# One encoder layer on one core: another tile order, another order of squares, scalings and loads in its output stage

## The reference, cut to what matters

```
u = rms_norm(x, g_norm);  z = u @ w_in             # q, k, v, g_att, xr, g_lru
o = diff_attention(q, k, v, ...)                   # 8 heads of 64
o_att = rms_norm(o per head, sub_norm) * (1 - lam_init)
o_lru = rg_lru_branch(xr, ...)                     # recurrences both ways
mix = concat([o_att * silu(g_att), o_lru * silu(g_lru)])
h = x + mix @ w_out
e = (p @ w_ple) * sigmoid(h @ w_pg)
y = h + rms_norm(e, g_ple)
```

## Time and profile before

| | |
|---|---|
| median of 3 runs | 1027.68 us (1026.09 to 1029.2) |
| the profiled execution | 1027.9 us, of which the span of the trace is 1026.1 us |
| granted TensorE clock, mean over the span | 0.993 |
| busy: PE / DVE / ACT / POOL | 97% / 66% / 62% / 47% |

### The profile page before, as it was taken

The page is one execution under the profiler, slowest core; times in us unless marked ns, Lnnn a source line. Parts: engine busy times, 40 slices in busy tenths (PEclk is TensorE's granted clock), DMA queues, the critical chain, the costliest instruction groups (busy, mean ns, idle before and its releaser), DMA issues.

```text
span 1026.1 us, 15666 instructions
## 1 busy us (share of the span) xinstructions
PE 990.3 (97%) x5720; PEld 785.2 (77%) x5720; DVE 679.0 (66%) x1117; ACT 636.8 (62%) x1051; POOL 482.8 (47%) x396
## 2 busy tenths in 40 slices
PE   8999999999999999989999999999989999999996
PEld 7867777777788888878777777777767887777775
DVE  4735857592583341579999999999848672444444
ACT  7748485846631231569999999999737443444442
POOL 1163343626656540155677676665610125555451
PEclk9999999999999999999999999999989999999999
DMA  9741543323255437659867666523457780222221
GB/s 345 273 142 36 174 149 104 118 82 134 72 177 184 142 95 204 212 158 234 208 195 173 149 188 173 132 93 124 171 168 239 230 280 10 72 74 81 86 73 68
DMA packets 106909, 154.55 MB, mean 151 GB/s; under 512 B 10313, under 2 KB 69193, under 8 KB 106825
## 3 DMA queue, kind: packets, MB, share of 16 engines
q1 hardware_dynamic: 106688, 153.55, 50.0%
q10 hardware_dynamic: 144, 0.00, 0.0%
HBM read 104.17 MB, written 46.20 MB: 147 GB/s over the span
## 4 chain that ended last, share of the span: by engine, by line
PE 66%; DVE 17%; issue 10%; ACT 3%; POOL 2%; DMA 2%; DVEq 0%; POOLq 0%; SPq 0%; ACTq 0%
DVE E_ L1899 10%; PE b_ps L2340 6%; PE b_ps L2342 6%; PE b_ps L2341 6%; PE b_ps L2202 6%; PE b_ps L2204 5%; PE b_ps L2203 5%; PE o_ps L2397 3%; PE s_ps L2353 3%; PE w_ps L2314 3%; PE uT_ps L2277 2%; DVE ratio L1908 2%; PE left_ps L2527 2%; PE left_ps L2530 2%; PE left_ps L2529 2%
## 5 line engine op out<-in xcount | busy, mean ns | idle before, releaser
L1381 ACT ACTIVATE E_<-E_,nmax 128x1024 f32<-128x1024 f32 (+1 forms) x184 | 186.6, 1018 | 13.2 <-DVE nmax L1899 13.2
L1899 DVE CUSTOM_DVE_ANT_0 E_<-s_ps,bias 128x1024 f32<-128x1024 f32 (+1 forms) x184 | 188.2, 1057 | 9.2 <-PE s_ps L2353 9.0
L1087 POOL TENSOR_TENSOR E_<-E_,ratio 128x576 f32<-128x576 f32 (+3 forms) x92 | 84.7, 920 | 92.6 <-DVE E_ L1915 92.6
L1090 POOL TENSOR_TENSOR E_<-E_ 128x576 f32<-128x576 f32 (+3 forms) x92 | 103.6, 1126 | 7.2
L2204 PE MATMUL b_ps<-u_hi,wA_lo 128*128 128x512 f32 x256 | 99.8, 390 | 0.0
L2353 PE MATMUL s_ps<-KL,QL 128*128 128x512 f32 x256 | 88.6, 430 | 8.1 <-DVE nmax L1899 8.0
L1396 ACT ACTIVATE WT<-w_ps 128x1024 f32<-128x1024 f32 (+1 forms) x96 | 83.5, 870 | 5.9 <-PE w_ps L2314 5.5
L2314 PE MATMUL w_ps<-ident,E_ 128*128 128x128 f32 x624 | 83.5, 273 | 2.1 <-ACT WT L1396 2.0
L2202 PE MATMUL b_ps<-u_hi,wA_hi 128*128 128x512 f32 x216 | 85.5, 396 | 0.0
L2314 PEld LDWEIGHTS w_ps<-ident,E_ 128*128 128x128 f32 x624 | 72.5, 140 | 15.2 <-issue 6.3
L2203 PE MATMUL b_ps<-u_lo,wA_hi 128*128 128x512 f32 x216 | 84.1, 389 | 0.0
(11 more groups left out here) (345 smaller groups left out, 2595.8 us busy)
## 6 DMA issues: line engine op xcount, KB each, us to landing
QL<-qk_t SPq DMA_DIRECT2D x32, 256.0 KB, 7.2
KL<-qk_t SPq DMA_DIRECT2D x32, 256.0 KB, 8.5
bias<-line_d SPq DMA_DIRECT2D x8, 960.0 KB, 12.1
x_sb<-in_x SPq DMA_DIRECT2D x12, 512.0 KB, 9.0
z_ch<-z_stage SPq DMA_DIRECT2D x24, 256.0 KB, 3.2
qk_t<-qh SPq DMA_DIRECT2D x24, 256.0 KB, 2.3
qk_t<-ql SPq DMA_DIRECT2D x24, 256.0 KB, 2.8
mf<-mix_t SPq DMA_DIRECT2D x24, 256.0 KB, 4.8
```

Of the source, the lines that this page charges most:

```text
L1090: gp.tensor_tensor(one, one, two, ALU.add).then_inc(w_gp, 1)
L1381: act.activation(e, e, ACT.Exp, bias=nmax[:, n % 5, c:c + 1], scale=-1.0, accum_out=sums[:, n % 5, c:c + 1]).then_inc(e_done, 1)
L1899: dve.tensor_tensor_reduce(weights_at(n)[:, c, 0:n_tok], s_ps[:, c, 0:n_tok], b[:, ::-1], -1.0, 3e38, ALU.add, ALU.min, nmax[:, n % 5, c:c ...
```

## The change

Places 2 and 3 swap tiles, so place 2 is now tile 2, a short and a `HALF` tile, and the banks follow. SP loads it before it stores the last attention output, and in each round issues `load_mix` ahead of `load_o`. ACT squares `n + 3` at the head of its round, and scales `n + 2` after `mix_high(n + 1)`, with the root just before; the small root that was there to have the table loaded is gone. In places 4, 6 and 8 PE transposes the next tile behind the `half_tile` products instead of ahead of them. POOL makes `sums_low(0)` ahead of the low parts of p, and one low part of w_ple ahead of its last `add_half`. In the gate loop DVE makes `joined(g - 1, 3)` ahead of `scaled_e(g - 1, 1)`. In the last pair the gain goes to another buffer and no longer waits for the square, and one sum is put off.

```
@@ -382,7 +382,7 @@
         wo_hi_done = sem("wo_hi_done"); wl_lo_done = sem("wl_lo_done"); wa_lo_done = sem("wa_lo_done")
         wg_in = [sem(f"wg_in{s}") for s in range(2)]
         wp_in = sem("wp_in"); wp_hi_done = sem("wp_hi_done"); wp_lo_done = sem("wp_lo_done")
-        SEQ = [0, 1, 8, 2, 9, 3, 10, 4, 11, 5, 6, 7]
+        SEQ = [0, 1, 2, 8, 9, 3, 10, 4, 11, 5, 6, 7]
         WHOLE = [SEQ.index(t) for t in range(8, NT)]
         HALF = [i for i in range(NT) if i not in WHOLE]
         IN_DRAM = NT - 4
@@ -458,8 +458,8 @@
 
         def mix_bank(i):
 
-            if i < 3:
-                return (h_ps[:], hq_ps[:], all_ps[:, 4:8:3, :])[i]
+            if i < 4:
+                return (h_ps[:], hq_ps[:], h_ps[:], all_ps[:, 4:8:3, :])[i]
             return h_ps[:] if i % 2 else hq_ps[:]
 
         ORDER = [PAIRS - 2, PAIRS - 1] + list(range(PAIRS - 2))
@@ -935,15 +935,16 @@
             for b in range(2):
                 sp.wait_ge(hp_out[b], 16 * IN_STEPS // 2)
             load_x_again(1)
+            load_o(2)
             store_o(1, HEADS // 2 - 1)
-            sp.wait_ge(o_st[1], 16 * 4)
-            load_o(2)
             load_mf(10)
             for n in range(NT):
+                if n + 2 < NT:
+                    load_mix(n + 2)
+                if n == 0:
+                    sp.wait_ge(o_st[1], 16 * 4)
                 if n + 3 < NT:
                     load_o(n + 3)
-                if n + 2 < NT:
-                    load_mix(n + 2)
                 if 1 <= n < NT - 1:
                     load_x_again(n + 1)
                     if n + 1 in HALF and HALF.index(n + 1) >= 2:
@@ -1117,15 +1118,19 @@
                 gp.tensor_tensor(hp_sb[:, k % 2, :], hp_sb[:, k % 2, :], x_rd[n % 2][:], ALU.add
                                  ).then_inc(fin["x_sum"], 1)
 
+            def embedding_low(k):
+                gp.wait_ge(wp_hi_done, k + 1)
+                gp.tensor_tensor(wp_lo[:, k, :], wp_raw[:, k, :], wp_hi[:, k, :].bitcast(F32),
+                                 ALU.subtract).then_inc(wp_lo_done, 1)
+
             o_scale(0)
             add_half(0)
             o_scale(1)
             for k in range(1, len(HALF)):
+                if k == len(HALF) - 1:
+                    embedding_low(0)
                 add_half(k)
-            for k in range(PC):
-                gp.wait_ge(wp_hi_done, k + 1)
-                gp.tensor_tensor(wp_lo[:, k, :], wp_raw[:, k, :], wp_hi[:, k, :].bitcast(F32),
-                                 ALU.subtract).then_inc(wp_lo_done, 1)
+            embedding_low(1)
 
             def sum_low(g, i, raw, pair):
                 gp.wait_ge(fin["s_hi"], 4 * g + i)
@@ -1154,10 +1159,10 @@
                 gp.tensor_tensor(e_sb[:, r, :], e_sb[:, r, :], h_sb[:, slot_of(g, r), :], ALU.add
                                  ).then_inc(fin["y_done"], 1)
 
+            sums_low(0)
             gp.wait_ge(fin["x_sum"], len(HALF))
             p_low(0, 1)
             p_low(0, 0)
-            sums_low(0)
             sum_low(0, 4, s4_raw, s4)
             for g in range(LAST):
                 if g:
@@ -1507,10 +1512,8 @@
 
             mix_high(0)
             heads_out(2 * HEADS - 1)
+            square_o(2)
             mix_high(1)
-            act.activation(mse[:, 0:1], neghalf[:, 0:1], ACT.Sqrt, scale=-2.0)
-            square_o(2)
-            root_o(2)
 
             def a21_copy(g):
                 act.wait_ge(fin["h_tr"], START["h_tr"] + 4 * g + 1)
@@ -1558,17 +1561,19 @@
                 act.activation(p_hi[:, r, :, :], p_sb[:, r, :, :], ACT.Copy).then_inc(fin["p_hi"], 1)
 
             for n in range(NT):
+                if n == 0:
+                    root_o(2)
+                    scale_o(2)
+                if n + 3 < NT:
+                    square_o(n + 3)
                 if 1 <= n < NT - 1:
                     mix_high(n + 1)
-                if n + 2 < NT:
+                if 1 <= n < NT - 2:
+                    root_o(n + 2)
                     scale_o(n + 2)
-                if n + 3 < NT:
-                    square_o(n + 3)
                 if n in (0, 1, 2, 3, 4, 6, 8):
                     gate_high({0: 0, 1: 1, 2: 2, 3: 3, 4: 4, 6: 5, 8: 6}[n])
-                if n + 3 < NT:
-                    root_o(n + 3)
-                if n == NT - 2:
+                if n == NT - 3:
                     for k in range(PC):
                         act.wait_ge(wp_in, 32)
                         act.activation(wp_hi[:, k, :], wp_raw[:, k, :], ACT.Copy).then_inc(wp_hi_done, 1)
@@ -2008,6 +2013,11 @@
                     row = x_rd[n % 2][:]
                 if n >= 4:
                     dve.wait_ge(fin[f"h_out{n % 2}"], 16 * min(n // 2, 4))
+                if n == 3:
+                    dve.tensor_tensor(h_sb[:, n, LEFT], mix_bank(n)[:, 0, :], row[:, LEFT], ALU.add)
+                    dve.tensor_tensor(h_sb[:, n, RIGHT], mix_bank(n)[:, 1, :], row[:, RIGHT], ALU.add
+                                      ).then_inc(fin["h_done"], 1)
+                    return
                 dve.tensor_tensor(h_sb[:, n % 4, :].rearrange("p (a b) -> p a b", a=2), mix_bank(n),
                                   row.rearrange("p (a b) -> p a b", a=2), ALU.add).then_inc(fin["h_done"], 1)
 
@@ -2061,9 +2071,9 @@
             mix_low(0)
             o_normalise(1)
             heads_scaled(2 * HEADS - 1)
+            mean_square(2)
             o_gate(1)
             mix_low(1)
-            mean_square(2)
             for n in range(NT):
                 if 1 <= n < NT - 1:
                     o_gate(n + 1)
@@ -2134,6 +2144,7 @@
             for g in range(PAIRS):
                 if g:
                     joined(g - 1, 3, "p2", right_ps[:], sg[0][:, LEFT])
+                    scaled_e(g - 1, 1)
                     gated_e(g - 1, 0)
                     scaled_e(g - 1, 0)
                 joined(g, 1, "p7", left_ps[:], sg[1][:, RIGHT])
@@ -2147,7 +2158,6 @@
                 gated_e(g, 1)
                 sum_four(g + 1)
                 a12_low(g + 1)
-                scaled_e(g, 1)
 
             def half_e(k, r, c, sigs):
                 dve.wait_ge(fin["sig"], 4 * LAST + sigs)
@@ -2157,18 +2167,18 @@
                                   ALU.mult).then_inc(fin["e_done"], 1)
 
             def half_gain(k, r, c):
-                dve.wait_ge(fin["esq"], 2 * LAST + k)
-                dve.tensor_tensor(e_sb[:, r, c], e_sb[:, r, c], gpB[:, c], ALU.mult).then_inc(fin["t_done"], 1)
+                dve.wait_ge(fin["e_done"], START["e_done"] + 2 * LAST + k)
+                dve.tensor_tensor(sg[r][:, c], e_sb[:, r, c], gpB[:, c], ALU.mult).then_inc(fin["t_done"], 1)
 
             def last_mean(r, one, two):
                 dve.wait_ge(fin["esq"], 2 * LAST + two)
                 dve.tensor_scalar(mse[:, r:r + 1], sse[:, 2 + one:3 + one], sse[:, 2 + two:3 + two], EPS, ALU.add,
                                   ALU.add).then_inc(fin["ems"], 1)
 
-            def last_sum(r):
+            def last_sum(r, parts):
                 dve.wait_ge(fin["ers"], START["ers"] + 2 * LAST + r + 1)
-                for c in (RIGHT, LEFT):
-                    dve.scalar_tensor_tensor(out=e_sb[:, r, c], in0=e_sb[:, r, c], scalar=rse[:, r:r + 1],
+                for c in parts:
+                    dve.scalar_tensor_tensor(out=e_sb[:, r, c], in0=sg[r][:, c], scalar=rse[:, r:r + 1],
                                              in1=h_sb[:, slot_of(LAST, r), c], op0=ALU.mult, op1=ALU.add
                                              ).then_inc(fin["y_half"], 1)
 
@@ -2182,11 +2192,12 @@
             half_gain(3, 0, LEFT)
             half_e(4, 1, LEFT, 4)
             dve.wait_ge(fin["t_done"], 2 * LAST + 3)
-            last_sum(0)
+            last_sum(0, (RIGHT,))
+            half_gain(4, 1, LEFT)
             last_mean(1, 1, 4)
-            half_gain(4, 1, LEFT)
+            last_sum(0, (LEFT,))
             dve.wait_ge(fin["t_done"], 2 * LAST + 4)
-            last_sum(1)
+            last_sum(1, (RIGHT, LEFT))
 
 
         @block.tensor
@@ -2468,11 +2479,12 @@
                 if n == 1:
                     pe.wait_ge(wt_done, NSTEP)
                     pe.wait_ge(o_done, 2 * HEADS)
-                if n >= 3:
-                    pe.wait_ge(fin["h_done"], 1 if n == 3 else n - 1)
+                if n == 2 or n >= 4:
+                    pe.wait_ge(fin["h_done"], {2: 1, 4: 2, 5: 3}.get(n, n - 1))
                 if n in WHOLE[1:]:
                     half_tile(2 * SEQ[n])
                     half_tile(2 * SEQ[n] + 1)
+                    turn_o(n + 1)
                 pe.wait_ge(fin["m_lo"], n + 1)
                 for b in range(2):
                     c = slice(b * 512, (b + 1) * 512)
@@ -2598,7 +2610,8 @@
             pe.wait_ge(wa_lo_done, LC)
             mix_product(0, second_tile)
             for n in range(1, NT - 1):
-                turn_o(n + 1)
+                if n not in WHOLE[1:]:
+                    turn_o(n + 1)
                 mix_product(n)
```

18 lines of the change are left out of this document (9 added, 9 removed).

## The result

The changed kernel takes 1041.08 us (median of 4 runs, 1036.87 to 1041.88), the one before 1027.33 us (4 runs, 1026.09 to 1029.2): a ratio of 1.0124, 95% interval 1.0092 to 1.0156. The lowest of the four, 1036.87, ran at a mean clock of 0.994 where the others had 0.989 or 0.990; as an estimate from these figures, 4 to 5 us less are lost at half clock, which is about the difference. It is slower, as forecast (1039.8). The profiled execution took 1040.5 us with a span of 1038.8, 12.7 us more than before.

A forecast was written before the change was run, and what follows sets the result against it. PE, busy for nearly the whole span, was taken as the bound. 1027.9 + 18.6 (tile loop, start's gain included) - 3.5 (start of the gate loop) - 3.0 (gate loop) = 1040.0, median 1039.8; range 1031 to 1048.

The forecast's parts named there:

- The tile loop: Tile loop: each transpose is chained to the one before through the o_in transfer; a loss of 18.6 us.
- 5.1 + L: Tile loop: us from one transpose to the next, L being the load's landing, taken as 3.7; 8.8 in all.
- change nothing by themselves: Tile loop: transposes moved behind `half_tile` bring nothing, as PE sets the long interval; worth 2.8 us each were the chain over 11.5.
- The start: Place 2: `load_o(2)` issued earlier lets `turn_o(2)` start at 762.4 and not 764.97; a gain of 2.6 us.
- The assumption that the table load goes ahead of the wait in front of the root: ACT before `scale_o(2)`: the 1.28 us table load does not wait for what the root waits for.
- The start of the gate loop: Start of the gate loop: `sums_low(0)` first on POOL removes PE's 2.2 us wait and 1.7 of slow clock; gain 3.5 us.
- the second `s_lo` is there as PE wants it: Start of the gate loop: with `sums_low(0)` first on POOL, PE's 2.2 us wait for `s_lo` goes.
- The gate loop: Gate loop: `scaled_e` moved behind `joined` removes PE's five waits for `sg`, 2.6 us in all; gain 3.0, from 2.6 to 3.4.
- The end: Last pair: the moved gain already lies under POOL's root, the others under PE's last products; nothing gained.
- rival 1: Tile loop: loads land in 2.8 us, five chained intervals shrink by 0.9; 1035, or 1030 if the clock stays up; chance 0.13.
- The third rival: Tile loop: the transfer is hidden, 5.1 + L stays below PE's 6.0, no interval stalls; faster, 1018; chance 0.10.
- a stall of two microseconds or more is paid nearly twice: PE: a long wait also drops the clock to 1.2 GHz, costing about 2.1 or 1.7 us more.

The follow-up runs named there:

- The swap alone: Kernel before with only the tiles of places 2 and 3 swapped and what belongs to it, all other orders as before; 1026.87 us, ratio 0.9997.
- The ends alone: Kernel before with only the parts behind the tile loop changed: POOL's order, `joined` ahead of `scaled_e`, the last pair; 1021.98 us, ratio 0.9953.
- `joined` alone: Kernel before with only `scaled_e(g - 1, 1)` moved behind `joined(g - 1, 3)`; 1023.5 us, ratio 0.9966.
- the variant without reload: Changed kernel without the loads of o_in for places 4 to 11, orders as changed; 1022.14 us, ratio 0.9943.

## Why the prediction was right

**The tile loop** was right in its mechanism and nearly in its size. The chain was put at 5.1 + L; the rows above give 5.2 + 3.05. Leaving the transfer out took the loss away, delaying it made it larger, undoing either order took 12.1 and 10.4 us of it away. That the moved transposes "change nothing by themselves" held in the changed kernel, but not once the orders were restored: there `turn_o(11)` waited 1.8 us, for `o_gate(9)` had come late and pushed DVE's two weight passes into the next round. That is read from the trace; it was not tried alone. The moved transposes alone do not make this wait: with them and the square at the head of ACT's round, the two variants whose load was early or left out have none at `turn_o(11)`.

Two sizes in the loop were off, each with errors of both signs that nearly cancelled, which is luck. From the issue of the load to the square, L was 3.0 in three of the five intervals that the chain sets (to `turn_o(3)`, (6) and (10)), 3.9 and 4.4 in the others (to `turn_o(4)` and `turn_o(8)`), for my 3.7. And the slow clock came elsewhere than I had put it: behind the wait at `turn_o(4)` (13.1 us to the next transpose, where I had 11.5), not behind that at 8 (11.6 where I had 13.2).

The 2.6 us that the prediction took from the Trainium skill ("DMA: Bandwidth & Descriptors", Anatomy of one DMA) come from a fit that the page gives for transfers issued by GpSimd, and o_in goes through SP's queue. No load of these five intervals was that quick.

**The start** was over-sized: 1.5 us and not 2.6. The step that failed is the landing of `load_o(2)`, 5.0 in my sum and 5.6 measured (5.7 to 6.8 in the variants that issue it in the same place), with `o_gate(1)` held back by it: it came at 758.41 for 757.11 before, 1.3 us late where I allowed 0.3. The sum had a slip besides, 755.7 where 750.9 + 5.0 is 755.9. The assumption that the table load goes ahead of the wait in front of the root was not put to the test here: DVE's reciprocal was ready at 758.5, and ACT came to the table load at 759.84. The swap alone gave nothing measurable.

**The start of the gate loop** gave less than 3.5. The slow clock behind the wait did go, 1.7 us, but the wait fell only from 2.2 to 1.6. The failing step is "the second `s_lo` is there as PE wants it"; it is also the one sign of those I had named that did not come. POOL's timeline after:

```profile
860.02 4.51 POOL L1118 TENSOR_TENSOR hp_sb<-hp_sb,x_rd 128x1024 f32<-128x1024 f32 x1 [5.09 <-DMA hp_sb<-hpart]
864.49 2.38 POOL L1123 TENSOR_TENSOR wp_lo<-wp_raw,wp_hi 128x1024 fp32r<-128x1024 f32 x1
866.84 2.40 POOL L1118 TENSOR_TENSOR hp_sb<-hp_sb,x_rd 128x1024 f32<-128x1024 f32 x1
869.20 2.41 POOL L1123 TENSOR_TENSOR wp_lo<-wp_raw,wp_hi 128x1024 fp32r<-128x1024 f32 x1
871.56 3.77 POOL L1137 TENSOR_TENSOR s_lo<-s_raw,s_hi 128x512 fp32r<-128x512 f32 x3
```

POOL is never idle from 860.0 on. The `add_half` at 860.02 took 4.5 us for the usual 2.4; a weight pass of DVE ran from 860.00 to 862.28. And both low parts of w_ple still stand ahead of `s_lo`. Which of the two keeps the wait was not tried; the 2.1 us that this `add_half` took too long are by themselves more than the 1.6 us of the wait. So the gain is 0.6 + 1.7 = 2.3 us. The ends alone less `joined` alone, both against the same runs of before, is 0.9953 against 0.9966: 1.3 us, with intervals that overlap.

**The gate loop** was right: 3.0 forecast, and `joined` alone gave 0.34%, 3.5 us (2.3 to 4.7). In the changed kernel the new wait of 0.7 us takes part of it back. **The end** was not run alone.

**The rivals.** Quick landing (3.0) happened in three rounds. Over the five chained intervals it makes 1.2 us less than with my 3.7, where rival 1 wanted 4.5, and the clock fell behind three of the waits (at `turn_o(3)`, (4) and (6)) all the same. The third rival's condition holds in the variant without reload: it gives 1022.1 where I had 1018; the 4 us are the start, which kept a wait of 4.4 us and its slow clock, the rest of the wait for `s_lo` (1.1 us) and the new one of 0.7 us.

## What to carry to other kernels

Before an instruction is moved to the head of an engine's round, ask what it waits for, and when that is issued: an in-order queue turns a harmless late load into a wait for all that stands behind. Two orders on two queues may each cost a little (3.5 and 5.2 us here) and together close a cycle that costs more than their sum, so look for the loop from one round's result through a queue back to the next round's input, add its terms up, and hold the sum against the bounding engine's shortest round, not its mean. And ahead of a load, count what the queue has sent just before: 256 KB landed in 3.0 to 4.4 us right behind one load of the same size, and in 6.5 behind 1.5 MB.

## What the hardware did that I had not expected

A long wait does not always cost clock. Windows of the changed kernel (busy us of PE, PEld, DVE, ACT, POOL, granted clock, DMA share, GB/s):

```profile
784.00:790.00 6.00, 5.26 (x18) 4.28 (x19) 4.22 (x5) 2.50 (x4) 0.00 (x0) 0.72 0.44 116
806.00:812.00 6.00, 5.91 (x21) 4.82 (x22) 3.61 (x3) 1.84 (x2) 2.39 (x1) 0.72 1.06 328
828.00:834.00 6.00, 5.21 (x25) 4.31 (x26) 4.28 (x5) 2.54 (x5) 2.40 (x1) 1.00 0.52 181
848.00:854.00 6.00, 5.47 (x26) 4.53 (x27) 5.90 (x5) 3.05 (x6) 1.97 (x1) 1.00 0.77 312
```

Waits of 2.3 us (at 784.74) and 2.0 us (at 806.09) were followed by a mean clock of 0.72 over six us, which at the two levels of 2.4 and 1.2 GHz costs 1.7 us in each; waits of 3.4 us (at 828.79) and 2.0 us (at 848.53) by none at all. The Trainium skill ("TensorE: Matmul & The Clock Gate", Part 1) lets the clock depend on how busy the engine was over a past stretch and not on the length of one wait; these rows agree with that as far as the length alone does not decide. What did decide in these four cases was not tried. So the prediction's "a stall of two microseconds or more is paid nearly twice" does not hold as a rule: two of these four stalls were, two were paid once.

The order of the instructions alone does not decide it either, since the executions of the changed kernel differ in their mean clock (0.989 to 0.994).
